# A gated token-mixer layer on eight cores: tiles worked in pairs, with one causal convolution per 1024 tokens

## The reference, cut to what matters

```
h = rmsnorm(x);  z = h @ w_in           # columns: u | v | a | gl | gate_a | gate_b, 1024 each
A: u = gelu(u); v = layernorm(gelu(v))
   mix = per group of 128 channels: tril(W_s) (128x128) over the tokens of a chunk
   y_a = (u * mix) @ w_a_out
B: glu = a * sigmoid(gl)
   c = causal_dwconv(glu, 31 taps) ; c = silu(layernorm(c)) ; y_b = c @ w_b_out
x += (sigmoid(gate_a)*y_a + sigmoid(gate_b)*y_b) @ w_o
h = rmsnorm(x); up = causal_dwconv(h @ w_up, 3 taps); x += (gelu(gate)*val) @ w_down   # 5632 / 2816 wide
x += rmsnorm(p @ w_ple) * sigmoid(rmsnorm(x) @ w_pg)
out = rmsnorm(x)
```

## Time and profile before

| | us |
|---|---|
| median of 3 runs (4795.12 to 5013.43) | 4795.77 |
| the profiled execution's own time | 4797.65 |
| span of its slowest core (core 2) | 4795.4 |
| spans of all cores | 4762.7 to 4795.4 |
| PE busy in the span | 4560.8 |
| DVE busy | 3029.4 |
| ACT busy | 2162.4 |

### The profile page before, as it was taken

How to read it: one execution, slowest core, us unless ns; L and a number is a source line. 1 busy time by engine, 2 the same in 40 slices (tenths; PEclk the granted TensorE clock), 3 DMA queues, 4 the chain that set the end, 5 groups by cost and what they waited for, 6 DMA issues and landing times.

```text
span 4795.4 us, 82884 instructions; the slowest of 8 cores (4762.7 to 4795.4 us)
## 1 busy us (share of the span) xinstructions
PE 4560.8 (95%) x26261; PEld 2297.2 (48%) x26756; DVE 3029.4 (63%) x5086; ACT 2162.4 (45%) x4240; POOL 910.8 (19%) x1559
## 2 busy tenths in 40 slices
PE   6898799999999999999999999999999999999998
PEld 3444344445454454545445454554545445454553
DVE  4565675665766657575675766657575665766557
ACT  2244154453545445354453545445254453545444
POOL 1140040120302103030120302112030220302112
PEclk9989899999999999999999999999999999999999
DMA  9997996536474464646536464463645546464452
GB/s 176 173 177 184 229 225 207 214 141 229 163 239 161 157 239 143 226 174 201 195 145 225 172 232 165 159 234 138 234 174 195 198 142 232 166 229 165 161 211 101
DMA packets 279433, 902.87 MB, mean 188 GB/s; under 512 B 88160, under 2 KB 168416, under 8 KB 192224
## 3 DMA queue, kind: packets, MB, share of 16 engines
q1 hardware_dynamic: 168384, 830.91, 49.5%
q0 software_dynamic: 73760, 58.23, 9.4%
q10 hardware_dynamic: 36864, 8.40, 1.0%
HBM read 857.12 MB, written 81.79 MB: 196 GB/s over the span
## 4 chain that ended last, share of the span: by engine, by line
PE 70%; DVE 9%; issue 6%; ACT 6%; DMA 6%; ACTq 1%; POOL 0%; DVEq 0%; another core or an unknown queue 0%; SPq 0%; POOLq 0%
PE ps L426 64%; PE ps L689 5%; ACT arena L458 3%; DMA arena<-w_in 2%; DVE arena L738 1%; DMA arena<-w_up 1%; PE ps L453 1%; DMA arena<-w_o 1%; DVE arena L794 1%; DVE arena L642 1%; DMA arena<-w_down 1%; DVE arena L701 1%; DVE arena L383 1%; DVE arena L580 1%; ACTq L620 1%
## 5 line engine op out<-in xcount | busy, mean ns | idle before, releaser
L426 PE MATMUL ps<-arena 128*128 128x512 bf16 (+2 forms) x18961 | 4158.4, 376 | 150.3 <-DMA arena<-w_in 27.2
L426 PEld LDWEIGHTS ps<-arena 128*128 128x128 bf16 x19456 | 1871.6, 98 | 2327.3 <-issue 290.4
L895 DVE SCALAR_TENSOR_TENSOR arena<-ps,arena 128x511 f32<-128x511 f32 x704 | 524.4, 745 | 131.6 <-ACT arena L892 119.9
L898 DVE SCALAR_TENSOR_TENSOR arena<-ps,arena 128x510 f32<-128x510 f32 x704 | 527.0, 749 | 76.8 <-DVE arena L895 4.6
L431 ACT ACTIVATE arena<-arena 128x1024 bf16<-128x1024 f32 x256 | 274.3, 1072 | 580.5 <-DVE arena L940 369.4
L892 ACT ACTIVATE arena<-ps,arena 128x512 f32<-128x512 f32 x704 | 505.0, 765 | 30.1 <-PE ps L426 29.9
L907 POOL TENSOR_TENSOR arena<-arena 128x512 bf16<-128x512 f32 x352 | 448.3, 1274 | 67.0 <-ACT arena L905 14.8
L905 ACT ACTIVATE arena<-arena 128x512 f32<-128x512 f32 x352 | 221.6, 630 | 501.2 <-POOL arena L901 500.5
L435 POOL TENSOR_TENSOR arena<-arena 128x1 f32<-128x1 f32 x256 | 140.8, 556 | 1534.5 <-DVE arena L433 1534.5
L458 ACT ACTIVATE arena<-ps,arena 128x128 bf16<-128x128 bf16 x1536 | 412.5, 425 | 10.7 <-PE ps L453 10.7
L781 ACT ACTIVATE arena<-ps 128x512 f32<-128x512 f32 x256 | 149.6, 599 | 537.1 <-DVE arena L794 265.6
(11 more groups left out here) (82 smaller groups left out, 2777.2 us busy)
## 6 DMA issues: line engine op xcount, KB each, us to landing
arena<-wscr SPq DMA_DIRECT2D x634, 1024.0 KB, 6.5
wscr<-arena SPq DMA_DIRECT2D x44, 1024.0 KB, 10.0
arena<-x SPq DMA_DIRECT2D x64, 512.0 KB, 9.0
out<-arena SPq DMA_DIRECT2D x16, 2048.0 KB, 17.5
arena<-wscr SPq DMA_DIRECT2D x29, 768.0 KB, 4.3
arena<-w_in POOLq DMA_DIRECT2D x20, 1024.0 KB, 25.5
arena<-w_up POOLq DMA_DIRECT2D x32, 512.0 KB, 31.8
arena<-p SPq DMA_DIRECT2D x16, 512.0 KB, 7.1
```

The lines of the kernel that those rows point to most:

```text
L426: e.matmul(_o, lhsT=_l, rhs=_r, start=_s, stop=_t))
L895: P.op("dve", (lambda e, acc=acc, bk=bk, w1=w1: e.scalar_tensor_tensor(out=acc[:, 1:512], in0=bank(bk)[:, 0:511], scalar=w1, in1=acc[:, 1: ...
L898: P.op("dve", (lambda e, acc=acc, bk=bk, w0=w0: e.scalar_tensor_tensor(out=acc[:, 2:512], in0=bank(bk)[:, 0:510], scalar=w0, in1=acc[:, 2: ...
```

## The change

Tiles are worked in pairs, tile a and tile b of 1024 consecutive tokens, and the convolution is done once for the pair, in tile a.

- Phases of 8 tokens and 16 channels (`PH = 8`, `NU = 40`, `NCONV = 10`): `GP` has 64 groups of 16 channels with 128 octets of tokens and 4 columns of history. Each group takes five matmuls (L741 of the new kernel). The ten tap blocks are built once, in tile 0.
- `spread(h)` writes half of the channels as 8 DMAs of 128 KB to an HBM buffer `gsd`, and `gather(h)` reads it back with one DMA of 1 MB into `GP`.
- The order in tile a: `a_gl(0)` (a and gl of tile a), V, u0, mixing 0 to 3, `a_gl(1)` (a and gl of tile b), then u1 with all eight chunks, then the branches. Tile b has V, u, mixing and the branches, no convolution. The four a/gl blocks are loaded twice per pair, the tap blocks once. There are two `HT`; the norm of tile b's x moves into tile a's V and u stages.
- In branch A of tile a, `ln_apply(m)` and `ln_silu(m)` follow each m = 1 to 7 (phase 0 is done ahead of the branch). The transposes of the silu are 8 x 8 in branch B of tile a, after its four gates; they serve both tiles.
- Buffers are shared by stage (regions r1 to r4): `CO`, the product, silu, its transposes and the FFN hidden share r1; `GP`, `T1` and `PEN` share r2; u and the mixed u are one buffer.
- p is loaded by a casting DMA of POOL instead of a DMA and a DVE cast. Outputs are stored in four DMAs per tile instead of one.

```diff
-PH = 4
-NU = 36
-NCONV = 9
+PH = 8
+NU = 40
+NCONV = 10
...
+    glu_seq = ["a0", "l0", "a1", "l1"]
+    late_seq = ["ga0", "wa0", "ga1", "wa1", "gb0", "wb0", "gb1", "wb1"] + names[ids["o0"]:]
+    pair_seq = glu_seq + ["v0", "v1", "u0"] + glu_seq + ["u1"] + ["c%d" % i for i in range(NCONV)] + late_seq + \
+        ["v0", "v1", "u0", "u1"] + late_seq
...
+        def spread(h):
+            for q in range(8):
+                eng = "sp" if q % 2 == 0 else "act"
+                src = GSV[16 * q:16 * q + 16, :, h * 512:(h + 1) * 512]
+                dst = gsd_d[h, :, :, q, :].rearrange("i r n -> r i n")
...
+        def gather(h):
+            P.dma("gr%d" % h, (lambda e: e.dma_start(out=GP.ap[:, 32 * h:32 * h + 32, 4:132],
+                                                    in_=gsd_d[h].rearrange("i r q (c n) -> (i r) (q c) n", c=4))),
...
+        def a_gl(part, after):
+            HG = HTS[part]
...
+                    mm_group(bka, [(wa[:, kc, j * 128:(j + 1) * 128], HG.ap[:, kc, :]) for kc in range(8)], reads=[HG.r(), wra], tag="a")
...
-                        if m <= 1:
-                            conv_chunk(6 + m)
-                            if m == 1:
-                                conv_history()
-                                for jj in range(PH):
-                                    ln_j(jj)
-                        elif m <= 5:
-                            ln_apply(m - 2)
-                            if m == 5:
-                                for jj in range(PH):
-                                    ln_silu(jj)
+                        if ab == 0:
+                            if m >= 1:
+                                ln_apply(m)
+                                ln_silu(m)
+                        elif m < 4:
+                            fin_scale(m)
+                        else:
+                            fin_store(m - 4)
...
+            a_gl(1, after_b)
+            ub = get_block("u1")
+            u_group(ub, 4)
+            conv_chunk(0)
+            conv_chunk(1)
+            gather(1)
...
+            for g in range(4, 8):
+                conv_chunk(g)
+                mix_g(g)
+            P.op("pool", (lambda e: e.tensor_copy(out=GPH.ap, in_=GP.ap[:, :, 128:132])), reads=[GP.r()], writes=[GPH.r()])
+            for jj in range(PH):
+                ln_j(jj)
+            ln_apply(0)
+            ln_silu(0)
```

More of the change, by code:

```diff
@@ L23 @@
 NSLOT = 6
-NSTG = 2
 CV_GMIX, CV_GFFN, CV_GPG = 0, 8, 16
@@ L206, in build_nc @@
[L206 to L219, removed]
@@ new lines, in hm, with hm_r, gv_ap, gv_r @@
+    def hm(j):
+        return r1b[:, j % 8, (j // 8) * 512:(j // 8 + 1) * 512]
+    def hm_r(j0, n):
+        return [(r1 + (j % 8) * 4096 + (j // 8) * 1024, 1024) for j in range(j0, j0 + n)]
+    def gv_ap(ts):
+        i = 2 * (ts % 2)
+        return CO.ap[:, i:i + 2, 0:512]
+    def gv_r(ts):
+        i = 2 * (ts % 2)
+        return [(r1 + (i + k) * 4096, 2048) for k in range(2)]
+    r2 = alloc(64 * 132 * 2)
+    GP = buf([64, 132], BF16, r2)
+    T1 = buf([8, 512], F32, r2)
+    PEN = buf([4, 1024], F32, r2)
@@ L223, in build_nc @@
+    HBT = [buf([1024], BF16, r4 + 2048 * i) for i in range(2)]
+    GPH = buf([64, 4], BF16)
     PBF = buf([4, 256], BF16)
@@ new lines, in v_norm, with v_stage @@
+            nb = NBF.ap[:, ts, :].rearrange("p (h d) -> p h d", h=2)
+            P.op("dve", (lambda e, gv=gv, nb=nb, mv=mv, lv=lv: e.tensor_scalar(out=nb, in0=gv, scalar1=mv.ap[:, 0:1],
+                                                                             scalar2=lv.ap[:, 1:2], op0=ALU.subtract, op1=ALU.mult)),
+                 reads=gv_r(ts) + [mv.r(), lv.r()], writes=[NBF.r(ts)])
+        def v_stage(after):
+            vb = [get_block("v0"), get_block("v1")]
+            for ts in range(4):
+                v_ts(vb, ts)
+                if ts >= 1:
+                    v_norm(ts - 1)
+                after(ts)
+            v_norm(3)
+            release(vb[0][0])
+            release(vb[1][0])
@@ new lines, in spread @@
+        def spread(h):
+            for q in range(8):
+                eng = "sp" if q % 2 == 0 else "act"
+                src = GSV[16 * q:16 * q + 16, :, h * 512:(h + 1) * 512]
+                dst = gsd_d[h, :, :, q, :].rearrange("i r n -> r i n")
+                P.dma("g%s%d" % (eng[0], h), (lambda e, dst=dst, src=src: e.dma_start(out=dst, in_=src)),
+                      reads=gs_r(h), writes=[("gd", h, q)], eng=eng)
+            for q in range(8):
+                gsem = "g%s%d" % ("s" if q % 2 == 0 else "a", h)
+                P.lastw[("gd", h, q)] = (gsem, P.dcnt[gsem], "dma")
@@ L951, in build_nc @@
             release(n)
-        dn = [get_block() for _ in KB]
+        dn = [get_block("dn%d" % (3 + ki)) for ki in range(3)]
         for ts in range(4):
@@ L955, in build_nc @@
             for (k0, nk), (n, wv, wr) in zip(KB, dn):
-                mm_group(bk, [(HMT.ap[:, k0 + kc, ts * 128:(ts + 1) * 128], wv[:, kc, :]) for kc in range(nk)],
-                         reads=[HMT.r(k0, nk), wr], first=(k0 == 0), last=(k0 == 16), tag="down")
+                mm_group(bk, [(hm(k0 + kc)[:, ts * 128:(ts + 1) * 128], wv[:, kc, :]) for kc in range(nk)],
+                         reads=hm_r(k0, nk) + [wr], first=(k0 == 0), last=(k0 == 16), tag="down")
                 if ts == 3:
```

538 lines of the change are left out of this document (296 added, 242 removed).

## The result

The changed kernel is slower: ratio 1.0755, 95% interval 1.0709 to 1.0801. The profiled execution took 5161.86 us against 4797.65, another one 5153.35. The forecast was 5059 (4950 to 5145): right in sign and in its largest term, about 100 us too low, and the time lies 8 to 17 us above the range. Two terms of the sum failed it: the convolution stage, priced at 3 us a pair, costs 13.9, and a wait in tile b that was put at nothing costs 5.7.

A forecast was written before the change was run, and what follows sets the result against it. PE's own instruction stream was taken as the bound. Per pair +28.1 us, times 8 is +225, plus 53 for tile a starts, minus 15 at the start: 5061 from 4797.65, forecast 5059 us (4950 to 5145).

The forecast's parts named there:

- largest term: Layernorm and silu of the convolution in branch A of tile a: PE waits 35.7 us per pair.
- Part 1: Convolution matmuls on PE: 320 instead of 576 per pair at 0.056 us each, 14.3 us less per pair.
- Part 2: Branch A of tile a: sigmoid, layernorm, silu loop of 7.78 us a round; PE loses 35.7, 2.5 and 2.7 per pair.
- rivals on part 2: Branch A: load ahead of wait, 4977 us (0.12); no reload, 4905 (0.05); PE bound, 4708 (0.04); drain, 5236 (0.03).
- Part 3: Start of tile a: a_gl(0) needs all of HT, PE waits 4.9 us plus 2.7 for the clock, seven times.
- Part 4: Convolution stage: spread, gather and tap loads make PE wait 3 us per pair, bounds 0 and 12.
- late-DMA rival: Convolution stage: the DMA side costs 12 us per pair instead of 3, giving 5131 us; chance 0.10.
- tile b free of waits: Sign expected in the profile: PE has no waits in the second tile of a pair.
- part 5: Small items: PE's 0.8 us wait for DVE in a and gl goes, 1.5 us less per pair; the others zero.
- The start: Tile 0: ten tap builds on DVE instead of 18, taken as -15 us, between -45 and +20.

The follow-up runs named there:

- e1: Changed kernel with the eight silus of tile a in one run behind the last layernorm step; ratio to the kernel before 1.0241.
- e6: Changed kernel with the first six a and gl products of tile a computed in halves of 256 tokens; 621.4 us a pair against 627.6.
- e12: Changed kernel with the edits of e9, and all convolution matmuls reading the first tap block (wrong taps, nine loads left out); 4749.04 us.
- e5: Changed kernel with tile b's token mixing begun only after the fifth product of u, two groups at a time; 621.9 us a pair against 627.6.
- e9: Changed kernel with four edits together, those of e1, e3, e5 and e6; ratio to the kernel before 1.0085, 584.5 us a pair.
- e3: Changed kernel with gather(0) issued right behind spread(0), ahead of two weight loads; 628.0 us a pair against 627.6.

## Why the prediction was wrong

**Part 1, -14.3 a pair: right in the price.** 2560 matmuls, still 0.056 us each where PE doesn't wait (40 in 2.23).

**Part 2, +40.9: right.** The rounds are 7.75 and 7.78 us apart (2175.84, 2183.59, 2191.37), forecast 7.78. ACT in one round:

```profile
2179.19 1.28 ACT L776 ACT_TABLE_LOAD   x1 [3.59 <-DVE arena L771]
2180.48 1.06 ACT L776 ACTIVATE arena<-arena 128x1024 bf16<-128x1024 f32 x1
2181.56 1.28 ACT L845 ACT_TABLE_LOAD   x1
2182.85 0.60 ACT L845 ACTIVATE arena<-ps 128x512 f32<-128x512 f32 x1
```

From the end of the last convolution at 2134.3 to the silu's transposes at 2205.03 are 70.7, forecast 70.4, so PE loses 36.0 of them. From there to the first output matmul at 2212.11 are 7.1 us, with the 64 transposes at the low clock. Before, the two times 32 transposes of a pair took 2.0 us each (2301.86 to 2303.87), so this is 3.1 more; the forecast had 5.2. Together 39.1. e1 took back 33.0 and keeps 30.4 us of waits for silu and evictions on core 2, 3.8 a pair, and some clock behind them.

The rivals on part 2 fall. The load stands behind its instruction's wait (3.59 us idle, then the load), so it is not ahead; both loads are needed; PE does not cover the loop; and no drain shows: from the end of the silu at 2181.54 to the sigmoid at 2182.85 are 1.31 us, all but 0.03 of it the load. So the 1380 ns that the Trainium skill adds ("ScalarE: Activation LUTs", What ACT_TABLE_LOAD costs) do not show here, and its advice to batch calls by table set (the section on table sets) does: e1 is that advice, 5% of the kernel.

**Part 3, +7.6: a little high.** The wait was 4.79 as forecast, e6 gave back 6.2; the clock behind it cost 1.4 to 1.7 instead of 2.7.

**Part 4, +3 with bounds 0 and 12: the step that failed.** PE waits (78.0 + 3.5) / 8 = 10.2 us a pair for gathers and taps and runs at half clock behind two of the waits, 1.9 and 1.8 us more: 13.9, over the upper bound. I had compared bytes with time over the whole stage, "39 us for some nine blocks", and found 31 to 46 us. Two things were left out. The spread, its landing, the gather and its landing are a chain in series (17.7 us in e12 with no tap load in the way) with 13.5 us of cover. And the DMA engines carried nothing from 2068 to 2076, as I read it because no slot was free, so the demand fell into one burst: from 2080 to 2144 their share is 0.8 to 1.0 in the windows. The first half of the idle stretch (window):

```profile
2068.00:2072.00 4.00, 4.00 (x20) 1.84 (x19) 1.85 (x2) 0.60 (x1) 0.00 (x0) 1.00 0.00 0
```

The late-DMA rival had the right kind of miss and stopped at 12. My reason for 3, that "the stage of before had the same pressure and PE did not wait for weights", did not hold. That stage had no trip through HBM, and it spread its nine tap blocks over 38.6 us, from the first to the end of the last of its eight chunks (kernel before, timeline), where the changed kernel asks for ten in about 24 us of PE work:

```profile
2527.77 2.17 PE L689 MATMUL ps<-arena 128*128 128x128 bf16 x36
...
2564.35 2.17 PE L689 MATMUL ps<-arena 128*128 128x128 bf16 x36
2566.36 20.88 PE L426 MATMUL ps<-arena 128*128 128x512 bf16 x94
```

**Not in the sum: mixing and norms in their new places.** V's last norm in tile b: before, the mixing stood behind a and gl; in the changed tile b mix(0) follows the second product of u and waits 4.16 us for L632. I wrote "tile b free of waits" and had read the new order only in tile a. e5 gave back 5.7. And the norm of tile b's x, moved into tile a's V and u stages, makes PE wait there by 0.59, 0.84 and 1.15 us, 2.6 a pair. Where that norm stood before, at the end of the first tile, PE waited 0.5 us that it does not wait now, so 2.1 is the cost, which I had taken as zero.

**The pair, added up:** -14.3, 39.1, 6.2, 13.9, 5.7, 2.1 and -1.5 (part 5, not measured by itself) make 51.2, measured 53.7, so 2.5 us have no place. Some terms are core 2's in one pair and some are medians, and a sum can't be closer than that. Of the 18.0 us above the forecast of 35.7, the conv stage is 10.9, the mixing 5.7, the norms 2.1 and the open rest 2.5; parts 2 and 3 give 1.8 and 1.4 back.

**The start, -15: too small a saving.** By the same terms the first pair should have been 28.1 + 7.6 - 15 = 20.7 us longer (with the wait at its end); it is 13.2 shorter, 34 us off. The DMA engines are the bound there (share 1.02 from 0 to 631 us, PE busy 486), so waits of PE cost less: e1, worth 33.0 in a settled pair, begins tile 2 only 25 us earlier. How much of the 34 is this and how much are the eight tap builds less was not tried.

On core 2, by whose span 5161.86 came: six pairs 20 us too cheap each (2 of them that core's late gathers), 120; the last pair 16; the start -34. That is 102, the way from 5061 to about 5162. That the miss was not 136 us is luck: the start, which I had not understood, happened to err the other way. The range failed since its upper end held one late case (late DMA, 5131) and no second miss beside it.

## What to carry to other kernels

Work out a chain that alternates between two engines as one sum per round, table loads included, and set it against the cover per round: 7.78 against 3.45 us could be read before the run, and doing the silus in one batch was worth 5%. A write to HBM, a wait and a read back are a latency and not only bytes (17.7 us here, with other loads close behind): sum them apart from the bandwidth, and look whether full buffers leave the DMA engines idle just before; moving the gather in time moved the wait, and another ring changed nothing. When stages are reordered, read the start of every stage in every variant of the tile: two places that were not looked at, a wait of 4.16 us and three small ones, cost 7.8 us a pair.

## What the runs showed of the hardware that was not expected

A wait of 4 to 7 us costs PE 1.4 to 2.4 us on top, and the number of matmuls behind it does not decide how much: 8 matmuls of u behind the wait for L632 took 3.62 us instead of 1.89, 80 convolution matmuls 6.34 instead of 4.46 in the changed kernel and 6.89 in e12 (1931.66 to 1938.55, behind 4.25 us), 40 of them 4.02 instead of 2.23, and the 192 of `a_gl` 43.1 instead of 41.7. The 64 transposes behind the 7.30 us for the last silu took 6.38 us, and 3.98 in e9 behind 1.94 us. The 2.7 us that I took from tile 1 followed a wait of 9.75.

A gather of 1 MB in pieces of 256 bytes landed after 7.0 us with no load issued just ahead of it and two just behind (e3), and after 11.3 and 17.3 us among tap loads in the changed kernel. From POOL's ring the median was 12.4, from SP's 13.8.
